# Two of four prompt tiles multiplied with the whole expert table instead of gathering their rows

## The reference

```python
q = (xb @ w_q).reshape(TOK_BLK, PEER_HEADS, 2, DK_HALF)            # 8 heads, two halves of 128
s = jnp.einsum('thcd,hcnd->thcn', q, sub_keys)                      # 128 keys for each half
s1, i1 = lax.top_k(s[:, :, 0], TOPK); s2, i2 = lax.top_k(s[:, :, 1], TOPK)   # 16 each
cand = s1[..., :, None] + s2[..., None, :]                          # 256 sums, number i1 * 128 + i2
top_s, pos = lax.top_k(cand, TOPK)                                  # 16 of 16384 experts per head
g = softmax(top_s)
hid = gelu(einsum('thkd,td->thk', u_tab[eid], xb))                  # 128 rows of U per token
y = einsum('thk,thkd->td', g * hid, v_tab[eid])                     # 128 rows of V per token
```

## Time and profile before

| what | value |
|---|---|
| median of 3 timed runs (lowest, highest) | 1687.11 us (1685.46, 1694.51) |
| span of the profiled execution | 1709.3 us |
| busy: TensorE, VectorE, ScalarE, GpSimd | 82%, 64%, 37%, 38% |
| moved by DMA | 664.8 MB, mean 389 GB/s |
| of it by GpSimd's gathers | 571.75 MB |
| mean granted clock of TensorE | 0.956 |

### The profile page before, as it was taken

How to read it: one execution, slowest core, us unless ns; L and a number is a source line. 1 busy time by engine, 2 the same in 40 slices (tenths; PEclk the granted TensorE clock), 3 DMA queues, 4 the chain that set the end, 5 groups by cost and what they waited for, 6 DMA issues and landing times.

```text
span 1709.3 us, 17753 instructions
## 1 busy us (share of the span) xinstructions
PE 1404.9 (82%) x5164; PEld 622.7 (36%) x5164; DVE 1085.5 (64%) x2884; ACT 634.5 (37%) x1889; POOL 652.7 (38%) x703
## 2 busy tenths in 40 slices
PE   8999996768997978888878887777777777777786
PEld 5585663435333434334423232222223222222211
DVE  2459978868000046777766766666668888888654
ACT  2421113445211024344444454444445444444443
POOL 3034333322565653333333333333333333333332
PEclk9999996888998989999999999999999999999999
DMA  9798889999999999999999999999999999999997
GB/s 344 292 357 313 318 318 364 398 411 385 358 362 338 386 375 399 413 409 417 410 423 421 406 416 422 421 421 403 407 422 396 414 422 420 405 419 413 409 406 324
DMA packets 112144, 664.81 MB, mean 389 GB/s; under 512 B 13072, under 2 KB 14336, under 8 KB 52400
## 3 DMA queue, kind: packets, MB, share of 16 engines
q0 software_dynamic: 97824, 571.75, 83.4%
q1 hardware_dynamic: 14224, 91.93, 13.8%
HBM read 658.03 MB, written 5.60 MB: 388 GB/s over the span
## 4 chain that ended last, share of the span: by engine, by line
DMA 37%; PE 37%; issue 8%; ACT 7%; DVE 6%; another core or an unknown queue 3%; POOL 0%; ACTq 0%; SPq 0%; DVEq 0%; POOLq 0%
DMA area_r<-in_uv_tab,eid 36%; PE bank L907 11%; PE bank L627 9%; PE bank L851 4%; PE bank L896 4%; ACT area_c L1003 3%; PE bank L798 2%; DVE area_r L1703 2%; PE bank L558 1%; PE bank L871 1%; ACT L1253 1%; DVE area_x L1711 1%; DMA area_w<-in_w_in 1%; PE bank L767 1%
## 5 line engine op out<-in xcount | busy, mean ns | idle before, releaser
L907 PE MATMUL bank<-area_r,area_c 128*128 128x512 f32 (+1 forms) x1584 | 778.8, 624 | 213.8 <-ACT area_c L1003 212.8
L1873 POOL DMA_INDIRECT area_r<-in_uv_tab,eid x544 | 515.7, 948 | 944.0 <-PE bank L907 590.0
L1703 DVE CUSTOM_DVE_ANT_0 area_r<-area_r,bank 128x1024 f32<-128x1024 f32 x416 | 506.3, 1218 | 288.0 <-DMA area_r<-in_uv_tab,eid 287.3
L907 PEld LDWEIGHTS bank<-area_r,area_c 128*128 128x128 f32 (+1 forms) x1584 | 273.3, 188 | 713.0 <-issue 712.6
L1253 ACT ACTIVATE area_c<-hid 128x1 f32<-128x1 f32 x416 | 84.2, 202 | 538.8 <-DVE hid L1703 538.3
L1694 DVE CUSTOM_DVE_ANT_0 area_r<-area_r,bank 128x1024 f32<-128x1024 f32 x128 | 152.9, 1212 | 25.5 <-DMA area_r<-in_uv_tab,eid 22.7
L627 PE MATMUL bank<-area_w,area_t 128*128 128x384 f32 (+1 forms) x448 | 157.6, 509 | 4.1 <-DMA area_w<-in_w_in 3.5
L1003 ACT ACTIVATE area_c<-ident,area_c 128x128 f32<-128x128 f32 x364 | 146.1, 401 | 34.9 <-ACT area_c L1003 1.1
L1873 POOL DMA_INDIRECT area_r<-in_uv_tab,eidT x128 | 121.4, 948 | 82.0 <-issue 29.3
L1003 ACT ACTIVATE area_x<-bank 128x384 f32<-128x384 f32 (+8 forms) x123 | 49.9, 423 | 212.4 <-remote 59.4
L851 PE MATMUL bank<-area_t,area_w 128*128 128x416 f32 (+1 forms) x448 | 118.8, 418 | 6.1 <-issue 5.2
(11 more groups left out here) (200 smaller groups left out, 1202.6 us busy)
## 6 DMA issues: line engine op xcount, KB each, us to landing
area_w<-in_w_in SPq DMA_DIRECT2D x12, 1536.0 KB, 11.1
area_w<-in_k_cache SPq DMA_DIRECT2D x8, 1920.0 KB
area_w<-in_w_q SPq DMA_DIRECT2D x14, 1024.0 KB, 6.8
area_r<-in_uv_tab,eid POOLq DMA_INDIRECT x544
area_w<-in_w_out SPq DMA_DIRECT2D x4, 2048.0 KB, 11.6
area_w<-in_v_cache SPq DMA_DIRECT2D x4, 1920.0 KB
area_v<-in_v_cache SPq DMA_DIRECT2D x4, 1152.0 KB
area_x<-in_x_p SPq DMA_DIRECT2D x6, 512.0 KB
```

Of the source, the lines that this page charges most:

```text
L907: mm = pe.matmul(acc[0:n, c, :], diag[by_pe(i) % DG][:, 0:n], x_ring[s][:, D + c * 512:D + (c + 1) * 512], start=(i == 0), stop=False, ski ...
L1703: vec.tensor_tensor_reduce(out=u, in0=u, in1=x_cur, scale=1.0, scalar=0.0, op0=ALU.mult, op1=ALU.add, accum_out=hid[t % 2][:, j:j + 1]).th ...
L1873: nc.gpsimd.indirect_dma_start(out=ring[s], out_offset=None, in_=table, in_offset=bass.IndirectOffsetOnAxis(ap=where, axis=0)).then_inc(la ...
```

## The change

Tiles 2 and 3 (256 tokens, `DENSE`) no longer gather. All 16384 experts are gone through in 128 blocks of 128, twice. In the first pass SyncE loads a block of U (512 KB, ring of 4), TensorE multiplies it with the 256 tokens (`hidden`, 8 calls of 256 columns), ScalarE applies gelu and stores four blocks at a time to a scratch tensor in memory. Meanwhile the routing of tiles 2 and 3 ends in two key numbers per slot instead of an expert number; VectorE makes for each token a one-hot matrix of the first number times the gate (`make_firsts`), GpSimd one of the second without a gate (`make_seconds`), and TensorE multiplies the two (`build_weights`, four tokens at a time, 64 builds) to a 128x128 matrix, the gate of each expert for this token. ScalarE collects 32 tokens (2 MB, one staging buffer) and stores them to a second scratch tensor. In the second pass hidden values and gates are loaded again, VectorE multiplies them (`weigh_block`), and TensorE multiplies the product with a block of V (`add_block`, 4 calls of 512 columns).

Tile 1 and the samples keep their gathers (ring of 5), but VectorE adds all their V rows (`slot_add`), and its dots read x from SBUF. 78 of tile 1's slots lie in the first pass (`SLOTS_U`), 50 in the second (`SLOTS_V`), and the 32 sample slots in the second (`SLOTS_S`); the lists give the block at which each stands. All eight query jobs are computed before the first block, tile 0's last 20 V slots stand between the first ten blocks, and VR goes from 12 to 8. The tiles end in the order 0, 1, samples, 2, 3.

The core of the diff (new buffers, semaphores and the removed functions of the gathered path are left out):

```diff
-UR, VR, XR = 6, 12, 6
-DG = 4
+UR, VR, XR = 6, 8, 5
 RING = 3
 
...
+NBLK = N_EXPERTS // P
+GATHERED = 1
+DENSE = range(2, NT - 1)
+ND = len(DENSE) * P
+NBUF, NA = 4, 4
+HQ, HLOADS = 4, 3
+TB, WQN = 32, 8
+BUILT = 4
+NBUILD = ND // BUILT
+PER_TILE = P // BUILT
+PER_BATCH = TB // BUILT
+SAMPLE_SLOTS = SLOTS // GROUPS
...
-ROUTE_STEP = {g: [g + 2] for g in range(8, 24)} | {g: [2 * g - 22, 2 * g - 21] for g in range(24, 31)}
-JOBS_AHEAD = 3
+ROWS_AT = range(1, 10, 2)
+SUM_FIRST_AT, START_AT = 14, 20
+BUILD_AT = [45 + w * 6 // 5 for w in range(NBUILD)]
+EXP_AT = {1: 4, 2: 40, 3: BUILD_AT[PER_TILE] - 4}
+TURN_AT_BLOCK = {2: BUILD_AT[0] - 2, 3: BUILD_AT[PER_TILE] - 2}
+LINKS_FROM = {2: 4, 3: 42}
+LINKS_TO = {2: 40, 3: BUILD_AT[PER_TILE] - 4}
+SLOTS_U = [12 + i * 30 // 22 for i in range(22)] + [44 + 3 * i for i in range(12)] + [82 + i for i in range(44)]
+SLOTS_V = [1 + i * 3 // 2 for i in range(SLOTS - len(SLOTS_U))]
+SLOTS_S = [90 + i for i in range(SAMPLE_SLOTS)]
+LINKS_S_TO = 84
+GATES_S, Y_ONE_AT = 86, 88
+SAMPLE_SUM_AT = 126
+H_LOAD_AT, STORE_AT = 110, (20, 112)
+Y_ORDER = (0, GATHERED, SAMP) + tuple(DENSE)
+
...
+            def load_u(b):
+                sp.dma_start(blk[b % NBUF], u_blocks[b]).then_inc(blk_in[b % NBUF], 16)
+
+            def load_v(b):
+                sp.dma_start(blk[b % NBUF], uv_tab[b * P:(b + 1) * P, D:2 * D]).then_inc(blk_in[b % NBUF], 16)
+
+            def load_weights(m):
+                src = w_scratch[:, :, m * WQN * TB:(m + 1) * WQN * TB].rearrange("t p f -> p t f")
+                sp.dma_start(w_load[m % 2].rearrange("p t b k -> p t (b k)"), src).then_inc(w_load_sem[m % 2], 16)
+
+            def load_hidden(n):
+                sp.wait_ge(h_stored[n % 2], 16 * (n // 2 + 1))
+                sp.dma_start(h_in[n % HLOADS].rearrange("p q k -> p (q k)"), h_scratch[n]).then_inc(h_in_sem[n % HLOADS], 16)
...
+            for b in range(NBUF, NBLK):
+                sp.wait_ge(h_done, b - NBUF + 1)
+                load_u(b)
+                n = b - H_LOAD_AT
+                if 0 <= n < HLOADS:
+                    if n == 0:
+                        sp.wait_ge(route_link, (DENSE[-1] + 1) * HEADS * LINKS)
+                    load_hidden(n)
+            for b in range(NBUF):
+                sp.wait_ge(h_done, NBLK + b - NBUF + 1)
+                load_v(b)
+                if b == 1:
+                    sp.wait_ge(built, NBUILD)
+                    sp.wait_ge(w_stored, 16 * (ND // TB))
+                    load_weights(0)
+                    load_weights(1)
+            for b in range(NBUF, NBLK):
+                sp.wait_ge(v_used, b - NBUF + 1)
+                load_v(b)
+                n = (b - 1) // HQ + 2
+                if b % HQ == 1 and n < NBLK // HQ:
+                    sp.wait_ge(a_ready, HQ * (n - HLOADS + 1))
+                    load_hidden(n)
+                m = (b - 1) // WQN + 1
+                if b % WQN == 1 and 2 <= m < NBLK // WQN:
+                    sp.wait_ge(a_ready, WQN * (m - 1))
+                    load_weights(m)
+                if b in STORE_AT:
+                    store_y(STORE_AT.index(b))
...
+            def hidden(b):
+                pe.wait_ge(blk_in[b % NBUF], 16 * (b // NBUF + 1))
+                if b >= len(H_HALF):
+                    pe.wait_ge(gelued, b - len(H_HALF) + 1)
+                for k in range(KD):
+                    mm = pe.matmul(h_psum(b), blk[b % NBUF][:, k * P:(k + 1) * P], featT[:, k, DENSE[0] * P:DENSE[0] * P + ND],
+                                   start=(k == 0), stop=(k == KD - 1))
+                mm.then_inc(h_done, 1)
...
+            def build_weights(w):
+                pe.wait_ge(firsts_ready, w + 1)
+                pe.wait_ge(seconds_ready, w + 1)
+                out = build_half(build_at["weights", w])
+                for q in range(BUILT):
+                    mm = pe.matmul(out[:, q * P:(q + 1) * P], hot_second[w % 2][:, q, :], hot_first[w % 2][:, q, :],
+                                   start=True, stop=True)
+                mm.then_inc(built, 1)
+
+            def add_block(b):
+                pe.wait_ge(blk_in[b % NBUF], 16 * ((NBLK + b) // NBUF + 1))
+                pe.wait_ge(a_ready, b + 1)
+                for t in DENSE:
+                    for c in range(2):
+                        mm = pe.matmul(sums[t][:, c, :], a_blk[b % NA][:, dense_no(t) * P:(dense_no(t) + 1) * P],
+                                       blk[b % NBUF][:, c * 512:(c + 1) * 512],
+                                       start=False, stop=(b == NBLK - 1), skip_group_check=True)
+                    if b == NBLK - 1:
+                        mm.then_inc(tile_summed, 1)
+                if b < NBLK - 1:
+                    mm.then_inc(v_used, 1)
+
+            def sum_samples():
+                pe.wait_ge(gelued, NBLK)
+                start_sum(SAMP)
+                pe.wait_ge(eye_ready, 1)
+                pe.wait_ge(x_added, SLOTS + SAMPLE_SLOTS)
...
+            for i in range(HEADS, len(JOBS)):
+                half_queries(i, 0)
+                if i > HEADS:
+                    key_scores(i - 1)
+                weigh_first(4)
+                half_queries(i, 1)
+                weigh_first(4)
+            key_scores(len(JOBS) - 1)
+            for c in range(2):
+                pe.wait_ge(q_copied[c], len(JOBS))
+            pe.wait_ge(s_ready, len(SCORED))
+            for b in range(NBLK):
+                hidden(b)
+                if b in ROWS_AT:
+                    weigh_first(4)
+                if b == START_AT:
+                    start_sum(DENSE[0])
+                for t in DENSE:
+                    if b == TURN_AT_BLOCK[t]:
+                        turn_picked(t)
+                for w in range(NBUILD):
+                    if b == BUILD_AT[w]:
+                        build_weights(w)
+            pe.wait_ge(build_read, len(build_at))
+            start_sum(DENSE[1])
+            for b in range(NBLK):
+                add_block(b)
+                if b == SAMPLE_SUM_AT:
+                    sum_samples()
...
+            def gelu_block(b):
+                n = b // HQ
+                if b % HQ == 0 and n >= 2:
+                    act.wait_ge(h_stored[n % 2], 16 * (n // 2))
+                act.wait_ge(h_done, b + 1)
+                nc.scalar.activation(h_out[n % 2][:, b % HQ, :], h_psum(b), ACT.Gelu).then_inc(gelued, 1)
+
+            def store_hidden(n):
+                act.wait_ge(gelued, HQ * (n + 1))
+                nc.scalar.dma_start(h_scratch[n], h_out[n % 2].rearrange("p q k -> p (q k)")).then_inc(h_stored[n % 2], 16)
...
+            def read_built(w):
+                if w % PER_BATCH == 0 and w > 0:
+                    act.wait_ge(w_stored, 16 * (w // PER_BATCH))
+                act.wait_ge(built, w + 1)
+                r, k = build_at["weights", w], w % PER_BATCH * BUILT
+                copy(w_out_stage[:, :, k:k + BUILT],
+                     half(BUILD_HALF[r % len(BUILD_HALF)]).rearrange("p (q i) -> p i q", q=BUILT)).then_inc(build_read, 1)
+
+            def store_weights(m):
+                act.wait_ge(build_read, build_at["weights", (m + 1) * PER_BATCH - 1] + 1)
+                nc.scalar.dma_start(w_scratch[m], w_out_stage.rearrange("p i k -> p (i k)")).then_inc(w_stored, 16)
+
+            def weigh_slot(j):
+                c = j % SLOTS
+                gates, gated_by = (gate_one, one_gates) if j < SLOTS else (gate_grp, samp_gates)
+                act.wait_ge(hid_ready, j + 1)
+                nc.scalar.activation(bent[:, c:c + 1], hid[1][:, c:c + 1], ACT.Gelu).then_inc(bent_ready, 1)
+                if c == 0:
+                    act.wait_ge(gated_by, 1)
+                act.wait_ge(bent_ready, j + 1)
+                copy(w_col[:, c:c + 1], gates[:, c:c + 1], bent[:, c:c + 1]).then_inc(col_ready, 1)
+
...
+            def slot_dot(j):
+                r, c = j % XR, j % SLOTS
+                dve.wait_ge(x_landed[r], 16 * (j // XR + 1))
+                u = x_ring[r][:, 0:D]
+                vec.tensor_tensor_reduce(out=u, in0=u, in1=xn_tile[GATHERED] if j < SLOTS else x_samp, scale=1.0, scalar=0.0,
+                                         op0=ALU.mult, op1=ALU.add, accum_out=hid[1][:, c:c + 1]).then_inc(hid_ready, 1)
+
+            def slot_add(j):
+                v, c = x_ring[j % XR][:, D:2 * D], j % SLOTS
+                acc = x_tile[GATHERED] if j < SLOTS else acc_samp
+                dve.wait_ge(col_ready, j + 1)
+                if j == SLOTS:
+                    vec.tensor_scalar(acc, v, w_col[:, c:c + 1], None, ALU.mult).then_inc(x_added, 1)
+                    return
+                if j > 0:
+                    wait_apart(dve, x_added, j)
+                vec.scalar_tensor_tensor(out=acc, in0=v, scalar=w_col[:, c:c + 1], in1=acc,
                                          op0=ALU.mult, op1=ALU.add).then_inc(x_added, 1)
+
+            def slot(j):
```

(95 more changed lines are left out.)

459 lines of the change are left out of this document (205 added, 254 removed).

## The result

The changed kernel takes 1789.6 us (median of 4 runs, 1786.2 to 1795.6) against 1686.3 us before: 1.0615 times as long, 95% interval 1.058 to 1.065. The prediction was 1699 us, with a range of 1655 to 1755. It had the direction but not the size: +103 us where it put +12. The profiled execution, one of the four, has a span of 1790.5 us.

The account below looks back on a forecast made before the run. DMA bytes bound the old kernel's gather stretch; after the change TensorE becomes the bound. Its floor of 1679 us plus stalls of 8 + 6 + 16 + 6 + 6 = 42 gives 1721, times 0.987 = 1699 us; range 1655 to 1755.

Parts of the forecast that it names:

- The floor, 1679 us: Whole span by TensorE's work without stalls: first block at 686 us, hidden blocks to 1215, V blocks to 1672, tail 7.
- 7 groups x 1.87 = 13 us: Before the first query matmul: 44 V slots done instead of 72, so queries start 13 us earlier, at 539 us.
- (a): Hidden blocks 82 to 120: DMA needs 4.7 us a block against TensorE's 4.26; 8 us of stall, bounds 0 and 35.
- (b): V blocks 0 to 75: DMA needs 3.63 us a block against 3.51, plus 1 KB pieces; 6 us, bounds 0 and 30.
- (c): V blocks 84 to 121, a sample slot per block from 90: DMA 153 us against 130; 16 us, bounds 5 and 35.
- ScalarE: Staging buffer: the next read waits for a 2 MB store; seven waits of 0 to 5 us, taken as 6 us.
- VectorE: Hidden blocks 12 to 40: slots and routing need 3.7 us a block against 3.5; 6 us, bounds 0 and 20.
- GpSimd: One-hots for the builds: 0.3 to 0.6 us each, fitting beside the gathers' issue; no time taken.
- the rival's 1.2: Rival 3, GpSimd is late: 1.2 us a one-hot, 38 us more in 32 builds beside dense slots, 1736 us; chance 0.10.
- The factor 0.987: Whole kernel: timed median 1687.11 us over profiled span 1709.3 us before the change, multiplied onto the predicted span.
- mixed traffic is dearer: Rival 2: DMA moves 386 GB/s, 1 KB pieces at half rate; 1764 us at worst, 1745 with leads; chance 0.12.
- The leads hold: Rival 1: rows prefetched in slack blocks cover the dense stretches at 422 GB/s; 1669 us, faster; chance 0.36.

Follow-up runs that it names:

- late reads: ScalarE reads built weights up to two blocks later, against the changed kernel: 1777.1 us; added to the kernel with only three row gathers made (1647.4 us): 1639.1 us.
- no_rows_late: Changed kernel with only the first three gathers of tile 1's and the samples' rows, and ScalarE reading built weights up to two blocks later: 1639.1 us.
- short_math: Changed kernel with all gathers made, but each slot's dot and addition covering 32 of 1024 columns: 1799.9 us.
- even slots: Changed kernel with the same 160 slots spread evenly over the blocks and the samples' routing ended at 66 instead of 84: 1792.6 us.
- three_mended: Changed kernel with later reads of built weights, V-pass loads of weights and hidden values started by ScalarE, and another slot spread, sparser in hidden blocks 44 to 80: 1717.8 us.
- gates_apart: Changed kernel with the V pass's loads of weights and hidden values started by ScalarE instead of SyncE: 1758.8 us.
- both_mended: Changed kernel with evenly spread slots, V-pass loads of weights and hidden values started by ScalarE, and later reads of built weights: 1713.2 us.

## Why the prediction failed, step by step

The prediction has a floor by TensorE, a sum of stalls, and a factor. All three were off, in different directions: the floor too high, the stalls far too low, the factor needless.

**The floor, 1679 us: 41 us too high.** The kernel without rows and with late reads has almost no stalls and a span of 1637.6 us. The call prices stood well: V blocks ran at 3.43 us, four calls of 0.858 (0.865 taken); hidden blocks without builds ran at 3.45 us (3.51 taken), with builds at 4.23 (4.26 taken). The V pass took 443 us where 454 had been put, since handing over cost nothing. The hidden pass took 528.4 where 529 had been put, partly by luck: waits of 12 us stand there in place of the 10 us for handing over. The largest miss is the arrival: in the changed kernel the first hidden block came at 658.8 us, not 686. The queries began at 518.5 us instead of 539. The windows up to the first query show the reason: before, TensorE was busy 90.41 of 102 us there at clock 0.93, and in the last 36 us of it 28.01 at 0.82; after, 67.28 of 68 at 1.00.

```profile
450.00:552.00 102.00, 90.41 (x502) 35.08 (x494) 6.91 (x9) 15.52 (x32) 64.80 (x68) 0.93 0.94 342
...
516.00:552.00 36.00, 28.01 (x208) 12.16 (x202) 2.56 (x3) 4.93 (x14) 22.48 (x24) 0.82 0.93 326
```

```profile
450.00:518.00 68.00, 67.28 (x366) 27.49 (x365) 4.76 (x7) 12.33 (x27) 37.81 (x40) 1.00 0.83 293
```

The step "7 groups x 1.87 = 13 us" took away only the V slots' work at full clock; with them went 11 us of idle time and 10 us more of busy time, at least in part calls at the lower clock. The other 7 us are in the query jobs, which took 140 us instead of 147.

**The stalls, 42 us: about 152 in fact.** The changed kernel's span less that of no_rows_late, 1790.5 - 1637.6, is 153 us: hidden pass 584.9 - 528.4 = 57 us where 8 + 6 + 6 had been put; the V pass 529.1 - 443.0 = 86 where 6 + 16 had been put; the seam 11.1 us where 3 was, within its bounds. A floor 41 us too high and stalls 110 us too low leave the 70 us by which the span was missed. So the right direction was luck: from the floor as measured, the prediction's own stalls and factor give (1637.6 + 42) x 0.987 = 1658 us, faster than before. Term by term:

(a) *DMA in hidden blocks 82 to 120*, 8 us (0 to 35): rows cost 38 us in blocks 80 to 120. The bound was worked from bytes over rate. What it left out, by the chain above, is that a late row or weight makes VectorE late, and with it the one-hots, the build and TensorE, while the DMA engines then stand idle in their turn (share 0.88).

(b), (c) *V blocks*, 22 us (5 to 65): 86. This is the largest miss and the step that failed: a queue was summed as a rate. The prediction said that VectorE would stand between gathers and TensorE. It did not, as VectorE's own waits in this pass show:

```profile
DVE area_w L1894 <- PE bank L1011: 184.0, 82, 13.6
```

It waited 184 us for TensorE. The late ones were the V blocks themselves: of the 86 us, 66.3 are TensorE's waits for them, nearly all behind the weights in SyncE's queue, and the other 20 are calls at the lower clock after such waits (last section). The cover is three blocks, 10.3 us, and the blocks behind the weights landed after 12.9 us in the median, up to 25. A queue of their own for the weights took 37 of the 86 us (31 us of time). Order and full engines are needed together: without rows the same order made TensorE wait for no V block. The prediction had named the 1 KB pieces as an unknown cost in bytes and never asked what is queued behind them.

*ScalarE*, 6 us: the wait of the read for the store was named, with 5 us of cover and 11 of PSUM. Stores took 12.8 us in the median, 9 even without rows: inside the 5 to 15 us that it named, but over the 5 us of cover. ScalarE waited 61 us for them in seven waits. Part of that lay beside other losses; late reads gained 15.9 us in the hidden pass. The cover counted was that of the gelus. The slot's weight, also behind the read and with no cover, was left out.

*VectorE*, 6 us for its time in blocks 12 to 40: blocks 12 to 40 took 102.5 us against 98.4 without rows, 4 us. Right in size. Its time in blocks 80 to 120, worth up to 18 us by short_math, was not put down.

*GpSimd*, 0: right, though the one-hot took 0.82 us in the mean where 0.3 to 0.6 had been taken, and the rival's 1.2 was not reached.

**The two coupled terms.** Taken singly and together the edits show what a sum of stalls can't: the even slots are worth nothing alone but 25 us on top of the two others. A stall that is removed uncovers another if the resource behind it is nearly full, and DMA and TensorE need almost the same time here. In the prediction's own bytes the V pass moves 128 x 0.79 + 82 x 1.05 = 187 MB; at the 400 GB/s of three_mended's windows that is 468 us by DMA against 443 by TensorE. The difference, 25 us, is about what (b) + (c) put, 22 us. So the bytes were priced well. Missing were the other 61 us, since every buffer was let absorb the rest: the order in the queue (529.1 to 492.5 us by gates_apart) and the crowding of the slots (492.5 to 470.7 by both_mended, which also has 7 slots fewer in this pass).

**The factor 0.987: 22 us.** The profiled execution of before was 1.3% longer than the timed runs, that of after is not (1790.5 against 1789.6). In every execution on record with both numbers the span is 1.8 to 1.9 us below the timed value; the 1709.3 us are one execution longer than any of the timed ones of that kernel (the longest took 1697.2 us), and no ground for a factor. Why it was longer is not shown by any run here. By stages the span is 1721 - 27 (arrival) + 36 (hidden pass, 549 with its stalls) + 8 (seam) + 53 (V pass, 476 with its stalls) = 1791 us, and the whole miss of 91 us is 70 us of span and 22 of factor, less 1.

The rivals: "mixed traffic is dearer" (0.12) came nearest with 1745 to 1764 us, but for the wrong reason; the full engines moved 396 to 403 GB/s, near the 410 that had been taken, and the 1 KB pieces cost nothing by themselves. "The leads hold" (0.36) is refuted by the waits above. Of the prediction's signs, the pitches held up to block 80, ScalarE's waits for the store showed, and TensorE's waits for VectorE near V blocks 90 to 121 did not; a clock below 1.00, which it had named as a sign of being wrong, came (0.92 and 0.94).

Open: how the losses of hidden blocks 80 to 120 divide where they overlap; what of the 28 us by which both_mended's V pass still exceeds 443 is bytes; and why less arithmetic made the blocks behind the weights land later.

## What to carry to other kernels

When two resources come out within a few per cent of each other, don't take the larger of the two for the time. Each late transfer can cost both, so ask for every transfer how many us of buffer its consumer has, and what lies ahead of it in the same queue, before bytes are divided by a rate. A big load that is asked for early and a small one that is needed soon belong in different queues. A wait in an in-order engine costs what is queued behind it and on whose path that lies: here one read of a staging buffer stopped ScalarE, VectorE, TensorE and the next block in turn.

## What the runs showed of the hardware

**The clock after a wait.** After a wait of 4.3 us for a V block, which ended at 1604.20 us, TensorE ran at a mean granted clock of 0.55 for 3.8 us, nearly all of it at the lower level of 1.2 GHz, then at 1.00, the level of 2.4 GHz:

```profile
1604.20:1608.00 3.80, 3.80 (x5) 1.65 (x6) 0.00 (x0) 0.00 (x0) 0.00 (x0) 0.55 1.01 416
1608.00:1612.00 4.00, 4.00 (x10) 1.71 (x9) 2.36 (x4) 0.50 (x2) 0.00 (x0) 1.00 0.99 406
```

The first five records start 0.85 to 0.88 us apart, the later ones in these windows 0.43 after one of 0.51. In the V pass this makes TensorE busy 462.5 us instead of 443.0: nearly 20 of the 86 us are not waiting but calls at the lower clock after it. Without rows, where TensorE doesn't wait in that pass, its clock is 1.00 throughout. The prediction had priced no stall with this.

**Short DMAs beside full queues.** A V block of 512 KB lands after 4.6 us in the median without rows, 7.9 with them and 10.0 with the weights in another queue; the longest in the chain took 25.0 us. In the changed kernel the four behind each load of weights took 12.9 us in the median, the others 5.8. What decides is not the median but how many land later than the 10.3 us of blocks that TensorE still holds.
